# Heads of an attention layer: where a block's late transposes and the conversions wanted later stand in three engines' queues

## The reference

```python
kvu = (ckv @ w_ukv).reshape(B, Lk, N_HEADS, NOPE_DIM + V_DIM)
k_nope, v = kvu[..., :NOPE_DIM], kvu[..., NOPE_DIM:]
def block(args):                       # 128 queries at a time, 8 heads
    qn_b, qr_b = args
    s = einsum('bqhd,bkhd->bhqk', qn_b, k_nope) + einsum('bqhr,bkr->bhqk', qr_b, k_rope)
    p = softmax(s.astype(float32) * ATTN_SCALE, axis=-1)
    return einsum('bhqk,bkhd->bqhd', p, v)
o = ...                                # all blocks and heads, side by side
return o @ w_o
```

## Time and profile before

| | |
|---|---|
| three timed runs | 3474.29, 3479.03, 3485.82 us |
| their median | 3479.03 us |
| the profiled execution, its own time | 3489.05 us |
| its span, first to last instruction | 3487.1 us |
| mean granted TensorE clock over the span | 0.961 |
| TensorE busy | 3246.7 us, 93% of the span |
| VectorE, ScalarE, GpSimd busy | 51%, 27%, 5% |

### The profile page before, as it was taken

How to read it: one execution, slowest core, us unless ns; L and a number is a source line. 1 busy time by engine, 2 the same in 40 slices (tenths; PEclk the granted TensorE clock), 3 DMA queues, 4 the chain that set the end, 5 groups by cost and what they waited for, 6 DMA issues and landing times.

```text
span 3487.1 us, 48061 instructions
## 1 busy us (share of the span) xinstructions
PE 3246.7 (93%) x18847; PEld 3149.3 (90%) x18847; DVE 1782.4 (51%) x3001; ACT 956.1 (27%) x1337; POOL 164.2 (5%) x201
## 2 busy tenths in 40 slices
PE   6999999998999999999779789898869999999997
PEld 4999999997999999999779678888769999999996
DVE  8666888786333333334635555555544333333333
ACT  4333212124111111112312554554623111111114
POOL 3000000003000000001200000000000000000002
PEclk8999999998999999999889899999989999999998
DMA  6444433320111111111103100101001111111111
GB/s 213 136 153 141 119 102 105 105 91 29 38 46 43 41 39 44 40 42 46 43 23 128 57 30 17 33 14 38 13 12 31 43 42 42 42 42 42 42 42 61
DMA packets 272667, 210.25 MB, mean 60 GB/s; under 512 B 15102, under 2 KB 243756, under 8 KB 272572
## 3 DMA queue, kind: packets, MB, share of 16 engines
q1 hardware_dynamic: 260908, 163.50, 15.4%
q0 software_dynamic: 11664, 45.39, 3.7%
HBM read 185.10 MB, written 23.76 MB: 60 GB/s over the span
## 4 chain that ended last, share of the span: by engine, by line
PE 79%; DVE 12%; issue 4%; ACT 3%; DMA 1%; SPq 0%; POOL 0%; DVEq 0%; ACTq 0%; POOLq 0%
PE set L559 65%; PE set L1049 4%; PE set L1037 3%; PE turned L802 2%; DVE pa L2211 2%; DVE soft L2670 2%; PE set L636 1%; DVE tmp L2028 1%; DVE hlo L2037 1%; PE set L702 1%; DVE pah L2152 1%; DVE x L2005 1%; PE set L593 1%; PE turned L733 1%; DVE ptl L2685 1%
## 5 line engine op out<-in xcount | busy, mean ns | idle before, releaser
L559 PE MATMUL set<-hhi,whi 128*128 128x384 f32 x2856 | 660.6, 339 | 8.2 <-DVE wlo L1922 6.1
L559 PE MATMUL set<-hlo,whi 128*128 128x384 f32 x2856 | 655.3, 337 | 0.0
L559 PE MATMUL set<-hhi,wlo 128*128 128x384 f32 x2856 | 655.1, 337 | 0.0
L2229 DVE SCALAR_TENSOR_TENSOR x<-set,mod,x 128x128 f32<-128x128 f32 x744 | 413.2, 612 | 279.4 <-PE set L559 279.1
L559 PEld LDWEIGHTS set<-hhi,whi 128*128 128x128 f32 x2856 | 512.9, 190 | 9.1 <-issue 6.7
L559 PEld LDWEIGHTS set<-hlo,whi 128*128 128x128 f32 x2856 | 515.3, 190 | 0.0
L559 PEld LDWEIGHTS set<-hhi,wlo 128*128 128x128 f32 x2856 | 515.3, 190 | 0.0
L1922 DVE TENSOR_TENSOR wlo<-wraw,whi 128x1024 fp32r<-128x1024 f32 x193 | 235.5, 1221 | 464.6 <-ACT whi L1183 434.9
L1183 ACT ACTIVATE whi<-wraw 128x1024 fp32r<-128x1024 f32 (+1 forms) x207 | 214.1, 1035 | 657.0 <-PE set L559 654.2
L1183 ACT ACTIVATE tmp<-set 128x1152 f32<-128x1152 f32 x97 | 110.1, 1135 | 712.9 <-PE set L559 704.4
L559 PE MATMUL set<-ghi,whi 128*128 128x384 f32 x1296 | 294.9, 335 | 1.6 <-DVE x L2229 1.6
(11 more groups left out here) (238 smaller groups left out, 4182.1 us busy)
## 6 DMA issues: line engine op xcount, KB each, us to landing
wraw<-in_f_w_in SPq DMA_DIRECT2D x176, 256.0 KB, 3.0
adu<-in_ada_w SPq DMA_DIRECT2D x48, 512.0 KB, 6.0
wraw<-in_f_w_out SPq DMA_DIRECT2D x88, 256.0 KB, 3.1
wraw<-in_a_w_in SPq DMA_DIRECT2D x64, 256.0 KB, 3.1
v_scratch<-vst POOLq DMA_DIRECT2D x16, 576.0 KB, 3.0
vld<-v_scratch POOLq DMA_DIRECT2D x16, 576.0 KB, 4.5
q_scratch<-tmp POOLq DMA_DIRECT2D x16, 576.0 KB, 3.2
aldr<-in_ada_w SPq DMA_DIRECT2D x8, 1024.0 KB, 11.1
```

The lines of the kernel that those rows point to most:

```text
L559: last = nc.tensor.matmul(ps[:, b, 0:cols], w, m[:, b * cols:(b + 1) * cols], start=(i == 0 and p == 0), stop=(i == n - 1 and p == 2))
L2229: last = v.scalar_tensor_tensor(dst, src, k.mod[:, gate + n, c:c + 1], dst, ALU.mult, ALU.add)
```

## The change

TensorE: block 6's early transposes move ahead of the next head's keys products, and its late ones between the two halves of these. ScalarE and VectorE: block 6's early group is taken around block 8's maximum (ahead of the exponential on ScalarE, ahead of the reciprocal on VectorE), its late group right behind; in the last head too. The conversions that stood between rounds move into `between`: on ScalarE behind the early transposes of a round and ahead of its exponential, on VectorE to the end of the round. The queries' first third moves by this from behind round 1 into round 2, the second from behind round 4 into round 5, the two halves of `kv_split` (in the last head: the two splits) from behind rounds 2 and 3 into rounds 3 and 4. `o_split` moves from the end of the head to ahead of the exponential of the next head's block 0 (ScalarE) and behind its reciprocal (VectorE). No instruction is added or taken away.

```diff
--- before.py
+++ after.py
@@ -999,7 +999,7 @@
 
     KEY_CH = ((0, 480), (480, 944), (944, KEYS))
 
-    def keys_job(self, h):
+    def keys_job(self, h, late=None, off=0):
 
         k, nc, s = self.k, self.nc, KV_SLOT
         ps = self.open()
@@ -1009,6 +1009,8 @@
                 for b, (lo, hi) in enumerate(self.KEY_CH):
                     last = nc.tensor.matmul(ps[:, b, 0:hi - lo], w, m[:, n, lo:hi],
                                             start=(n == 0 and p == 0), stop=(n == CT - 1 and p == 2))
+            if n == 0 and late is not None:
+                self.turn_probs(late, True, off)
         self.close(last)
 
     def values_job(self, blocks):
@@ -1109,9 +1111,8 @@
         self.head_middle(h)
         if h == 1:
             self.unit_ready()
-        self.keys_job(1 - h)
         self.turn_probs(6, False, 1)
-        self.turn_probs(6, True, 1)
+        self.keys_job(1 - h, 6, 1)
         self.weighted_job(h, 2)
         self.turn_probs(7, False, 2)
         self.next_head_ready()
@@ -1713,11 +1714,19 @@
         if before:
             self.read_out(1 - h, 3)
 
-    def head_round(self, h, s, pair=-1):
+    def between(self, h, s, ahead):
+
+        if ahead and s in (2, 5):
+            self.queries_hi(s // 3)
+        if h == 1 and s in (3, 4):
+            self.kv_split(s - 3) if ahead else self.split()
+
+    def head_round(self, h, s, ahead, pair=-1):
 
         if pair != -1:
             self.eng.wait_ge(self.k.mm_done, self.J.at(1))
         self.turned(s, False)
+        self.between(h, s, ahead)
         self.exponentials(s + 2, 3)
         if pair != -1:
             self.read_out(h, pair)
@@ -1727,20 +1736,14 @@
 
     def head_middle(self, h, ahead):
 
-        self.head_round(h, 1)
-        if ahead:
-            self.queries_hi(0)
-        self.head_round(h, 2, 0)
-        if h == 1:
-            self.kv_split(0) if ahead else self.split()
-        self.head_round(h, 3, None)
-        if h == 1:
-            self.kv_split(1) if ahead else self.split()
-        self.head_round(h, 4)
-        if ahead:
-            self.queries_hi(1)
-        self.head_round(h, 5, 1)
+        self.head_round(h, 1, ahead)
+        self.head_round(h, 2, ahead, 0)
+        self.head_round(h, 3, ahead, None)
+        self.head_round(h, 4, ahead)
+        self.head_round(h, 5, ahead, 1)
+        self.turned(6, False)
         self.exponentials(8, 3)
+        self.turned(6, True)
 
     def weighted_read(self, h, pair):
 
@@ -1754,14 +1757,14 @@
         self.head_middle(h, True)
         self.queries_hi(2)
         self.keys_hi()
-        self.turned(6, False)
-        self.turned(6, True)
         self.normalise(8, 3)
         self.B.step()
         self.weighted_read(h, 2)
         self.turned(7, False)
         self.turned(7, True)
         self.turned(8, False)
+        if h == 1:
+            self.o_split()
         self.exponentials(0, 3)
         self.normalise(0, 3)
         self.B.step()
@@ -1769,14 +1772,10 @@
         self.exponentials(1, 3)
         self.normalise(1, 3)
         self.B.step()
-        if h == 1:
-            self.o_split()
 
     def last_head(self):
 
         self.head_middle(1, False)
-        self.turned(6, False)
-        self.turned(6, True)
         self.normalise(8, 3)
         self.weighted_read(1, 2)
         for s in (7, 8):
@@ -2550,7 +2549,14 @@
         if before:
             self.out_lo(1 - h, 3)
 
-    def head_round(self, h, s, pair=-1):
+    def between(self, h, s, ahead):
+
+        if ahead and s in (2, 5):
+            self.queries_lo(s // 3)
+        if h == 1 and s in (3, 4):
+            self.kv_split(s - 3) if ahead else self.split()
+
+    def head_round(self, h, s, ahead, pair=-1):
 
         self.maxima(s + 2, 3, 0 if pair == -1 else CTX if pair is None else 2 * P)
         self.turned(s, False)
@@ -2558,25 +2564,20 @@
         if pair != -1:
             self.out_lo(h, pair)
         self.turned(s, True)
+        self.between(h, s, ahead)
         self.B.step()
 
     def head_middle(self, h, ahead):
 
-        self.head_round(h, 1)
-        if ahead:
-            self.queries_lo(0)
-        self.head_round(h, 2, 0)
-        if h == 1:
-            self.kv_split(0) if ahead else self.split()
-        self.head_round(h, 3, None)
-        if h == 1:
-            self.kv_split(1) if ahead else self.split()
-        self.head_round(h, 4)
-        if ahead:
-            self.queries_lo(1)
-        self.head_round(h, 5, 1)
+        self.head_round(h, 1, ahead)
+        self.head_round(h, 2, ahead, 0)
+        self.head_round(h, 3, ahead, None)
+        self.head_round(h, 4, ahead)
+        self.head_round(h, 5, ahead, 1)
         self.maxima(8, 3, 0)
+        self.turned(6, False)
         self.inverse_sum(3)
+        self.turned(6, True)
 
     def weighted_read(self, h, pair):
 
```

## The result

Four runs of the changed kernel had a median of 3440.47 us (3432.94 to 3442.59), four of the kernel before beside them 3481.47 (3474.29 to 3485.82): a ratio of 0.988, 95% interval 0.9861 to 0.990. The forecast was 3437; the medians lie 41.0 us apart, and 41.6 were forecast. The profiled execution took 3441.09 us (span 3439.4). One of the twelve executions in experiment 2 took 8147.65 us, which no trace here explains; its ratio leaves it out.

What follows compares the result with a forecast made beforehand. TensorE, with 79% of the chain, was taken as the bound, and its waits also lowered its clock. Terms 36.0 - 4.5 + 6.4 - 2.2 + 5.9 = 41.6 us off the 3479.03 median gave 3437.4, range 3424 to 3460.

Steps and rivals of the forecast that it cites:

- Late transposes inside the keys: Seven heads, start of keys products to end of weighted products: 15.0 us each becomes 9.9, gain 36.0, bounds 22.7 and 42.7.
- K: In a head's replay, the time where the keys products started before the change; block 6's early transposes start there after it.
- first rival: Weighted products behind the keys stay at the low clock, 5.5 us each: 13.3 us less gain, 3451 us; chance 0.13.
- The full clock: Weighted products behind the keys run at clock 1.00, taking 3.6 us instead of 5.5, after a 0.95 us wait.
- queries_lo(0): Its 1.13 us on VectorE before block 5's maximum lengthens the wait before block 3's late pair: 4.5 us lost.
- second rival: ScalarE's moved copies delay every exponential they stand before, 0.82 us twice a head: 11.5 us and more, 3451; chance 0.12.
- the keys term: The 36.0 us gain forecast for seven stretches from the keys products' start to the weighted products' end.
- kv_split: One round later in three h = 1 heads, shortening waits at blocks 3 and 4: 6.4 us gained, bounds 0 and 11.6.
- o_split: Before block 0's exponential in three heads, it lengthens a TensorE wait of 1.02 us: 2.2 us lost, bounds 0 to 3.1.
- Last head: Moved splits and block 6's earlier differences shorten waits and spare a low clock: 5.9 us gained, bounds 2 and 8.
- The range: Span of whole-kernel times around the 3437 us forecast: 3424 to 3460 us.
- The rule weighed: Short, frequent stops swing the clock, so new waits inside the keys would leave the weighted products at the low clock.

Runs made afterwards that it cites:

- experiment 2: Changed kernel with block 6's transposes and softmax order put back, so only the conversions are moved: 3491.62 us, ratio 1.0023.
- Experiments 1: Changed kernel with all conversions put back, so only block 6's transposes and softmax order differ from the kernel before: 3434.63 us, ratio 0.9861.
- experiment 5: Changed kernel with queries' conversions back in their old places, with o_split's back, or with both: 3426.84, 3442.77 and 3418.09 us.
- experiment 7: Both kernels run once more, unaltered, for second traces: changed kernel 3433.24 us, kernel before 3478.6 us.
- experiment 4: Kernel before, with 14 unused products issued between block 6's early and late transposes in seven heads: 3466.97 us, ratio 0.9953.

## Why the prediction was right

*Late transposes inside the keys.* Right, and for the reason given: 36.5 us against 36.0. The replay put the end of the weighted products at K + 9.9 and the wait at 0.95; the timeline has 9.87 and 0.88, with the two query differences and the maximum in a row on VectorE as replayed. All seven weighted products take 3.6 us at 1.00, so the first rival falls. Experiments 1 and 4 split the gain: 13.9 us come in these stretches when the stall is only filled, the rest when it is gone. What the replay didn't ask is whether the wait inside the keys has to be there: its upper bound was 42.7 without that wait, and block 6 alone reaches 45.3.

*The full clock.* The result was right, and the reason given for it does not hold. I argued that 0.95 is far below a wait of 2.93 that leaves the clock alone. That wait leaves it alone in six of six cases of the kernel before, but in the kernel with block 6 alone all three are followed by 0.57 to 0.64, here in its windows:

```profile
2025.95:2029.95 4.00, 4.00 (x18) 3.61 (x19) 2.37 (x6) 3.74 (x8) 0.00 (x0) 0.62 0.14 50
2173.24:2177.24 4.00, 4.00 (x17) 3.64 (x18) 2.37 (x6) 3.50 (x7) 0.00 (x0) 0.57 0.11 41
2320.95:2324.95 4.00, 4.00 (x18) 3.57 (x19) 2.38 (x6) 3.52 (x8) 0.00 (x0) 0.64 0.13 50
```

*queries_lo(0).* Right: block 3's late pair waits 1.91 to 2.02 us in seven heads, where 1.9 was forecast, and the first stretch of the stage is 1.3 longer (1.1). The second rival, that the conversions cost more than the sum had, is refuted as a total, and its reason for the most part: ScalarE's waits for the maximum covered the copies (58.8 down to 39.5, experiment 5). But it pointed to the right place: queries and `o_split` together cost 22.4 us of stage (20.6 without the last head). Of these 68.76 - 60.02 = 8.7 lie inside the keys term, where the replay had the queries in the order of the work, but the sum gave them no price of their own.

*kv_split.* 4.6 gained instead of 6.4. The waits did better than forecast: 2.93 and 1.71 became 2.00 and less than 0.3. In the head whose clock held, the stretch is 2.41 shorter, three of which would be 7.2. In the other two it is 1.1 shorter: the clock fell behind the 2.00, and no term of the sum had a price for that.

*o_split.* The wait of 1.02 went to 1.55, not 1.8: 0.53 a head instead of 0.73. The stretches that hold it and a queries_lo(0) lost 5.0 (5.6).

*Last head.* 7.4 against 5.9. Block 6's part was too small (by experiment 1, 79.19 to 74.77, 4.4 us; forecast 2.1), the splits' too large (2.9; forecast 3.8): block 4's wait went down to 1.02, where I had it rise to 2.1. These differences are no larger than those between executions: the last head took 77.66 us in the second one of the kernel before and 70.19 in that of the changed kernel.

*The range.* The errors of the terms are -1.8, +0.6, -0.2, +1.5 and +0.5. They are small; that their sum is 0.6 is luck. The rule weighed, from the Trainium skill ("TensorE: Matmul & The Clock Gate", "A second HAM failure mode: psum-queue depth-cycling"), that short, frequent stops between groups make the clock swing, did not hold where I weighed it: the products behind the waits of 0.79 to 0.90 inside the keys ran at 1.00 in 14 of 14 cases of both executions. Behind the single waits of 2.00 us in experiment 7 the clock fell in four of six. The rule fits best where the stage opens: there waits of 1.18 to 1.20 and of 0.82 us follow each other, 0.8 us apart, and the 4 us behind the second are at 0.57 to 0.62 in all twelve executions. The kernel before is among them, so the prediction's sentence that its trace agrees with the rule only behind the long waits overlooked this place.

## What to carry to other kernels

When work is moved into a place that is about to become critical, price it against the schedule after the change: here pairs of differences of 0.56 us, moved out of idle time and ahead of a maximum, took back 16 to 20 of the 50 us that the main edit gives alone, and the page's sums of busy time show nothing of it. A change made of several moves is best run move by move, and the best one kept: 3418.09 instead of 3440.47. A TensorE stall of 3 us can be worth removing for two reasons, itself and the clock of the products behind it.

## What the hardware showed

- The clock behind a wait isn't decided by the wait's length alone. Over the heads, the 4 us behind a wait of 0.7 to 1.2 us were at 1.00 unless another wait had come just ahead, or came just behind as where the stage opens (the last head's end left out). Behind 1.9 to 2.0 us they were low in 9 of 35 cases (five executions of four kernels), 8 of these among the 15 of h = 1 heads. Behind 2.93 us it was 0 of 6 before, 3 of 3 with block 6 alone and 2 of 3 with the filled stall. Why the same wait of the same length differs between kernels stays open.
- A fall costs some 1.3 to 1.5 us when nothing waits behind it (48.73 and 48.80 against 47.46 us for an h = 1 stretch of the changed kernel; 2.04 and 2.07 against 0.60 for `o_split` in experiment 5), and nothing when a later wait takes it up: with block 6 alone those stretches take 49.86 to 49.88 us with the fall, and before the change 49.86 to 49.89 without.
- Useless products in a stall can pay: 13.9 us over seven stalls in experiment 4.
